# RWKV's triangular inverse by doubling: two chunks' products on four 64x64 tiles of TensorE, half of them written across the partition halves

## The reference, cut to what matters

```
def step(S, inp):
    r_t, w_t, k_t, v_t, kk_t, a_t = inp
    S = (S * w_t[:, :, None, :]
         - jnp.einsum('bhvk,bhk->bhv', S, kk_t)[..., None] * (kk_t * a_t)[:, :, None, :]
         + v_t[..., None] * k_t[:, :, None, :])
    return S, jnp.einsum('bhvk,bhk->bhv', S, r_t)
```

## Time and profile before

| | us |
|---|---|
| median of 3 runs | 1801.77 |
| lowest and highest | 1799.81, 1803.62 |
| profiled execution, device time | 1798.85 |
| its span, first to last instruction | 1797.2 |
| TensorE busy | 1711.3 (95%) |
| VectorE busy | 568.5 (32%) |
| ScalarE busy | 402.5 (22%) |
| mean granted clock of TensorE | 0.985 |

### The profile page before, as it was taken

The page is one execution under the profiler, slowest core; times in us unless marked ns, Lnnn a source line. Parts: engine busy times, 40 slices in busy tenths (PEclk is TensorE's granted clock), DMA queues, the critical chain, the costliest instruction groups (busy, mean ns, idle before and its releaser), DMA issues.

```text
span 1797.2 us, 27278 instructions
## 1 busy us (share of the span) xinstructions
PE 1711.3 (95%) x10992; PEld 1276.2 (71%) x10992; DVE 568.5 (32%) x1302; ACT 402.5 (22%) x899; POOL 125.5 (7%) x214
## 2 busy tenths in 40 slices
PE   7998899999999999999999989999999998999997
PEld 5675667677767777777766756676777676777775
DVE  1341464332024163330034314733220331533201
ACT  3221242131133231110132212412311332211101
POOL 1013000010010010000010130000000110000000
PEclk9999999999999999999999998999999999999999
DMA  9537222283447333333174272312734573343331
GB/s 350 172 116 253 112 96 72 71 319 118 149 148 307 126 123 141 134 132 126 68 254 162 84 255 106 119 49 83 298 126 144 194 274 119 118 141 131 131 117 50
DMA packets 64464, 273.54 MB, mean 152 GB/s; under 512 B 8529, under 2 KB 32530, under 8 KB 37074
## 3 DMA queue, kind: packets, MB, share of 16 engines
q1 hardware_dynamic: 51266, 208.57, 32.2%
q0 software_dynamic: 12512, 61.94, 9.2%
q10 hardware_dynamic: 560, 1.30, 0.2%
HBM read 262.58 MB, written 9.19 MB: 151 GB/s over the span
## 4 chain that ended last, share of the span: by engine, by line
PE 84%; DVE 6%; DMA 3%; issue 3%; ACT 3%; SPq 2%; POOL 0%; ACTq 0%; DVEq 0%; POOLq 0%
PE banks L815 42%; PE banks L844 15%; PE banks L766 5%; PE banks L822 5%; PE banks L799 4%; PE banks L873 3%; PE banks L763 3%; DVE work L1940 2%; PE banks L771 1%; DMA work<-in_ml_n 1%; PE banks L1072 1%; DVE o_branches L1940 1%; PE banks L1474 1%; PE banks L1493 1%; SPq L597 1%
## 5 line engine op out<-in xcount | busy, mean ns | idle before, releaser
L815 PE MATMUL banks<-h_normed,weight_ring 128*128 128x288 f32 x1888 | 459.4, 406 | 1.1 <-ACT h_normed L1558 1.1
L815 PEld LDWEIGHTS banks<-h_normed,weight_ring 128*128 128x128 f32 x1888 | 358.6, 190 | 100.5 <-ACT h_normed L1558 1.5
L844 PE MATMUL banks<-h_normed,weight_ring 128*128 128x288 f32 x1024 | 282.0, 419 | 4.6 <-ACT values_by_token L1723 4.6
L844 PEld LDWEIGHTS banks<-h_normed,weight_ring 128*128 128x128 f32 x1024 | 190.0, 192 | 61.1 <-ACT values_by_token L1723 7.0
L815 PE MATMUL banks<-work,weight_ring 128*128 128x288 f32 (+1 forms) x960 | 226.8, 399 | 1.8 <-issue 1.8
L815 PEld LDWEIGHTS banks<-work,weight_ring 128*128 128x128 f32 x960 | 182.2, 190 | 46.1 <-issue 2.6
L1940 DVE TENSOR_TENSOR squares<-squares 128x288 f32<-128x288 f32 (+2 forms) x40 | 20.3, 508 | 329.4 <-ACT squares L1596 329.3
L799 PE MATMUL banks<-h_normed,weight_ring 128*128 128x288 f32 x448 | 117.1, 411 | 2.3 <-ACT projected L1558 2.3
L1558 ACT ACTIVATE work<-banks 128x32 f32<-128x32 f32 (+8 forms) x142 | 55.9, 393 | 235.4 <-PE banks L766 62.0
L799 PEld LDWEIGHTS banks<-h_normed,weight_ring 128*128 128x128 f32 x448 | 82.2, 190 | 27.4 <-issue 4.3
L873 PE MATMUL banks<-h_normed,weight_ring 128*128 128x288 f32 x288 | 79.8, 434 | 20.9 <-DMA weight_ring<-in_w 13.8
(11 more groups left out here) (307 smaller groups left out, 1657.4 us busy)
## 6 DMA issues: line engine op xcount, KB each, us to landing
weight_ring<-in_w SPq DMA_DIRECT2D x171, 1024.0 KB, 4.8
work<-in_pool SPq DMA_DIRECT2D x112, 144.0 KB, 3.3
work<-in_mem_k POOLq DMA_DIRECT2D x12, 1024.0 KB, 11.6
work<-in_mem_v POOLq DMA_DIRECT2D x12, 1024.0 KB, 9.2
work<-in_pool POOLq DMA_DIRECT2D x64, 144.0 KB, 3.8
weight_ring<-in_pool SPq DMA_DIRECT2D x48, 144.0 KB, 3.0
projected<-in_mem_k POOLq DMA_DIRECT2D x4, 1024.0 KB, 25.6
projected<-in_mem_v POOLq DMA_DIRECT2D x4, 1024.0 KB, 5.8
```

Of the source, the lines that this page charges most:

```text
L815: last = mm(ps[:, bank, 0:width], block_of(first + k), rhs(k), start=k == 0, stop=k == n - 1)
L844: last = mm(ps[:, BANK[g], 0:N], block_of(t[2] + k), H[:, k, :] if t[0] == "gate" else O[:, 2 * n + k, :], start=k == 0, stop=k == t[3] - 1)
```

## The change

Both tiles' products of a level pair are issued together, and half of them go to the other half of the partitions, so that all four 64x64 tiles of the array are in use.

- `rw_x`: tile 0's products are written to their own half, tile 1's to the other half (`crossed`). ScalarE brings tile 1's X back with two copies of 64x256 instead of one of 128x256.
- `rw_y`: the products for T stay in their own half; those for the transpose are written to the other half, into bank 0 (tile 0) or 1 (tile 1). VectorE brings them back with two sums of 64x256 (`rw_turned_adds`), and T is summed by one of 128x256.
- the last level (`rw_y_last`): as `rw_x`, tile 1's products are written to the other half, and its sum onto T is made by two of 64x256.
- VectorE's order: the masks of the next two steps come first, then the transposes' four sums, then T's two, then `up_out`. `rw_x` waits for the transposes' sums (a new semaphore, `rw_tm`) and for both masks, `rw_y` for T's sums of the pair before.
- TensorE waits once, ahead of the loop, until banks 0 and 1 have been read (`rw_tokc`). The samples' step has functions of its own and does the same as before.

The number of products, their sizes and the mixing blocks between them stay.

```
                     def rw_x(level):
-                        j, i = RW_LEVELS[level]
-                        n, bank = min(TT[i][1], CH), RW_BANKS[i][0]
-                        pe.wait_ge(*at("rw_off", level + 1))
+                        for j, i in RW_LEVELS[level:level + 2]:
+                            pe.wait_ge(*at("rw_off", level + 1 + i))
+                        if level:
+                            pe.wait_ge(*at("rw_tm", level))
                         for h in range(4):
-                            for s in chunks_of(i):
-                                last = put(ps[s, bank, h * n:(h + 1) * n], r_off[i][s, h, 0:n], r_tm[i][s, h, 0:n])
-                        last.then_inc(S("rw_x"), 1)
+                            for s in chunks_of(0):
+                                for i, out in ((0, s), (1, crossed(s))):
+                                    last = put(ps[out, RW_BANKS[i][0], h * CH:(h + 1) * CH], r_off[i][s, h, :], r_tm[i][s, h, :])
+                                    if h == 3 and s.start:
+                                        last.then_inc(S("rw_x"), 1)
                     def rw_y(level):
...
+                        if level > 1:
+                            pe.wait_ge(*at("rw_t", level - 1))
                         for h in range(4):
+                            c = slice(h * CH, (h + 1) * CH)
                             for s in chunks_of(i):
...
+                                put(ps[s, RW_BANKS[i][1], c], r_x[i][s, h, :], r_tt[i][s, h, :])
+                                last = put(ps[crossed(s), i, c], r_tt[i][s, h, :], r_x[i][s, h, :])
+                        last.then_inc(S("rw_y"), 1)
+                    def rw_y_last(level):
+                        pe.wait_ge(*at("rw_xc", level + 2))
+                        pe.wait_ge(*at("rw_t", level))
+                        for h in range(4):
+                            for s in chunks_of(0):
+                                for i, out in ((0, s), (1, crossed(s))):
+                                    last = put(ps[out, RW_BANKS[i][1], h * CH:(h + 1) * CH], r_x[i][s, h, :], r_tt[i][s, h, :])
+                                    if h == 3 and s.start:
+                                        last.then_inc(S("rw_y"), 1)
...
                     for level in range(0, 10, 2):
                         rw_x(level)
-                        rw_x(level + 1)
                         mix(104 + 2 * level)
-                        rw_y(level)
-                        rw_y(level + 1)
+                        if level in RW_LAST:
+                            rw_y_last(level)
+                        else:
+                            rw_y(level)
+                            rw_y(level + 1)
                         mix(106 + 2 * level)
...  (ScalarE)
-                        copy(r_x[i][0:n, :, 0:m], ps[0:n, RW_BANKS[i][0], 0:4 * m].rearrange("p (h s) -> p h s", h=4), "rw_xc")
+                        src = ps[:, RW_BANKS[i][0], 0:4 * m].rearrange("p (h s) -> p h s", h=4)
+                        if i == 1:
+                            copy(r_x[1][0:CH, :, :], src[CH:P])
+                            copy(r_x[1][CH:P, :, :], src[0:CH], "rw_xc")
+                        else:
+                            copy(r_x[i][0:n, :, 0:m], src[0:n], "rw_xc")
...  (VectorE)
+                    def rw_turned_adds(level):
+                        j, i = RW_LEVELS[level]
+                        wait("rw_y", level + 1)
+                        for to, of in ((0, CH), (CH, 0)):
+                            half = r_tm[i][to:to + CH, :, :]
+                            tt(half, half, by_head(ps[of:of + CH, i, 0:4 * CH], CH), ADD, "rw_tm" if to else None)
...
-                    for level in range(10):
-                        rw_adds(level)
+                    for level in range(0, 10, 2):
                         if level < 8:
                             rw_offs(level + 2)
-                        if level in (1, 5):
+                            rw_offs(level + 3)
+                            rw_turned_adds(level)
+                            rw_turned_adds(level + 1)
+                        rw_adds(level)
+                        rw_adds(level + 1)
+                        if level in (0, 4):
                             up_out()
```

More of the change, by code:

```diff
@@ L248 @@
         (12, "rows_free"),
+        (8, "rw_tm"),
         (11, "rw_off rw_t rw_x rw_xc rw_y"),
@@ L1297, in chunks_of, with crossed @@
                         return [slice(0, NS)] if i == 2 else [slice(0, CH), slice(CH, P)]
+                    def crossed(s):
+                        return slice(CH - s.start, P - s.start)
                     def rw_x(level):
-                        j, i = RW_LEVELS[level]
-                        n, bank = min(TT[i][1], CH), RW_BANKS[i][0]
-                        pe.wait_ge(*at("rw_off", level + 1))
+                        for j, i in RW_LEVELS[level:level + 2]:
+                            pe.wait_ge(*at("rw_off", level + 1 + i))
+                        if level:
+                            pe.wait_ge(*at("rw_tm", level))
@@ L1308, in rw_y @@
                     def rw_y(level):
                         j, i = RW_LEVELS[level]
-                        n, bank = min(TT[i][1], CH), RW_BANKS[i][1]
                         pe.wait_ge(*at("rw_xc", level + 1))
+                        if level > 1:
+                            pe.wait_ge(*at("rw_t", level - 1))
                         for h in range(4):
+                            c = slice(h * CH, (h + 1) * CH)
                             for s in chunks_of(i):
-                                last = put(ps[s, bank, h * n:(h + 1) * n], r_x[i][s, h, 0:n], r_tt[i][s, h, 0:n])
-                            for s in () if level in RW_LAST else chunks_of(i):
-                                last = put(ps[s, bank, (4 + h) * n:(5 + h) * n], r_tt[i][s, h, 0:n], r_x[i][s, h, 0:n])
+                                put(ps[s, RW_BANKS[i][1], c], r_x[i][s, h, :], r_tt[i][s, h, :])
+                                last = put(ps[crossed(s), i, c], r_tt[i][s, h, :], r_x[i][s, h, :])
@@ new lines, in rw_x_samples, with rw_y_samples @@
+                    def rw_x_samples():
+                        pe.wait_ge(*at("rw_off", 11))
+                        for h in range(4):
+                            last = put(ps[0:NS, RW_BANKS[2][0], h * NS:(h + 1) * NS], r_off[2][0:NS, h, 0:NS], r_tm[2][0:NS, h, 0:NS])
+                        last.then_inc(S("rw_x"), 1)
+                    def rw_y_samples():
+                        pe.wait_ge(*at("rw_xc", 11))
+                        for h in range(4):
+                            last = put(ps[0:NS, RW_BANKS[2][1], h * NS:(h + 1) * NS], r_x[2][0:NS, h, 0:NS], r_tt[2][0:NS, h, 0:NS])
@@ L1338, in _ @@
                     mix(102)
+                    pe.wait_ge(*at("rw_tokc", 4))
                     for level in range(0, 10, 2):
                         rw_x(level)
-                        rw_x(level + 1)
                         mix(104 + 2 * level)
-                        rw_y(level)
-                        rw_y(level + 1)
+                        if level in RW_LAST:
[3 more added lines that the diff above has]
+                            rw_y(level + 1)
                         mix(106 + 2 * level)
@@ L1389, in _ @@
                     mix(148)
-                    rw_x(10)
+                    rw_x_samples()
                     mix(150)
-                    rw_y(10)
+                    rw_y_samples()
                     mix(152)
@@ L2316, in rw_offs, with by_head @@
                         j, i = RW_LEVELS[level]
+                        if 1 < level < 10:
+                            wait("rw_x", level - 1)
                         tt(tile_of(r_off, i), tile_of(r_at, i), mask(i, "level_c", 4, j), MUL, "rw_off")
+                    def by_head(ap, m):
+                        return ap.rearrange("p (h t) -> p h t", h=4)
+                    def rw_turned_adds(level):
[4 more added lines that the diff above has]
+                            tt(half, half, by_head(ps[of:of + CH, i, 0:4 * CH], CH), ADD, "rw_tm" if to else None)
                     def rw_adds(level):
@@ L2322, in rw_adds @@
                         wait("rw_y", level + 1)
-                        k = 4 if level in RW_LAST else 8
-                        tt(inverses(i, k), inverses(i, k), ps[0:n, RW_BANKS[i][1], 0:k * m].rearrange("p (k t) -> p k t", k=k), ADD, "rw_t")
+                        src = ps[:, RW_BANKS[i][1], 0:4 * m]
+                        if level == 9:
+                            for to, of in ((0, CH), (CH, 0)):
+                                half = r_tt[i][to:to + CH, :, :]
+                                tt(half, half, by_head(src[of:of + CH], m), ADD, "rw_t" if to else None)
+                        else:
+                            tt(tile_of(r_tt, i), tile_of(r_tt, i), by_head(src[0:n], m), ADD, "rw_t")
                     rw_masks(0)
```

## The result

The changed kernel takes 1793.14 us in the median of 9 runs (1790.95 to 1800.2), the kernel before 1801.77 us in 9 runs (1798.67 to 1807.03). The two medians lie 8.6 us apart. The ratio of the runs is 0.996 (95% interval 0.9946 to 0.9974): faster by 0.4%, which is 7.2 us, and between 4.7 and 9.7. The forecast was 1794.0 us, 7.8 us less than before; that the median lies only 0.9 us from it is finer than these runs can tell. The profiled execution after took 1792.38 us (span 1790.7), against 1798.85 (1797.2).

What follows compares the result with a forecast made beforehand. The doubling stage was taken as bounded by what TensorE issues: 6.44 us saved less 2.52 us of waits is 3.92 us per layer, 7.8 us over two layers, giving 1794.0 us; range 1789.5 to 1799.5.

Steps and rivals of the forecast that it cites:

- The products on four tiles: TensorE's X, Y and last Y groups shrink to 0.62, 1.09 and 0.62 us, saving 6.44 us per layer before waits.
- Rival 2: In X and Y, crossed products don't overlap with own-half ones, which keep 1.08 and 2.01 us; 1803.3 us, chance 0.07.
- The price of a half sum: A VectorE half sum of 64x256 before X costs as a whole one, 0.42 us, bounds 0.27 and 0.94.
- Rivals 3 and 4: VectorE's half sums cheaper, 0.27 us, giving 1789.9 (chance 0.05); or dearer, at 0.94 us giving 1812.5 (chance 0.05).
- The wait before X: TensorE, through Y and the mixing blocks, waits 0.39 us for VectorE's four half sums, four times per layer.
- The wait behind pair 4's `up_out`: Two `up_out` instructions at pair 4 delay VectorE's next masks and sums, 0.19 us more wait, once per layer.
- X to Y: ScalarE's three copies after X stay hidden with 0.27 us to spare; only the last Y waits, 0.35 us.
- `rw_bg`: After the last Y, TensorE waits 0.42 us for VectorE's one whole and two half sums.
- The sum: Gain of 3.92 us per layer, stage 22.28 us; 7.8 us over both layers, 1794.0 us against the median.
- Kept behind the stage: After the stage, TensorE's unchanged order and the transfers move along, so the whole gain is kept.
- Rival 5: Half or all of the gain is given back later by a transfer that doesn't move along; 1798 to 1802, chance 0.09.

Runs made afterwards that it cites:

- the uncrossed control: Changed kernel with every product written to its own partition half, same order, half copies and half sums; ratio 1.0004 to the kernel before, stage 27.24 us.
- Y alone: Kernel before with only Y crossed (half sums by VectorE), X as before; ratio 0.9963 to the kernel before, stage 23.19 and 22.70 us.
- X alone: Kernel before with only X crossed (half copies by ScalarE), Y as before; ratio 0.9974 to the kernel before, stage 24.69 and 24.43 us.
- the tile stored crossed: Changed kernel with tile 0's matrix and transposed inverse kept on the other half from `rw_pairs` on, X waiting on one semaphore; 1792.22 us, ratio 0.9939.
- the fastest kernel: As the tile stored crossed, with one mixing block behind X, three behind Y in full rounds, one moved ahead of `rw_bg`; 1787.81 us, ratio 0.9919.

## Why the prediction was right, step by step

- **The products on four tiles** (0.62, 1.09, 0.62 us; 6.44 per layer): 0.63, 1.09, 0.63. `rw_pairs` and the state products of the trace before were the right rows. Rival 2, the products of one row strip in turn, is refuted by the trace after and by the uncrossed control, which is 4.6 us slower in the stage. The prediction took 30 ns per record in the state products as a sign of two tiles side by side, and the row for one tile alone, which it lacked, is in the trace before: four products that all lie on one 64x64 tile, 8 records in 0.60 us (314.27 to 314.87), less the 0.15 are 56 ns per record.

```profile
314.27 0.67 PE L1362 MATMUL banks<-work 64*64 64x64 f32 x8
314.87 1.24 PE L844 MATMUL banks<-h_normed,weight_ring 128*128 128x288 f32 x4
```

  The Trainium skill's rule (TensorE: Matmul & The Clock Gate, "The mechanism"), of weight loads that overlap only for another row group, isn't what these traces show for 64x64 float32 tiles: the state products, of one row group and two column groups, went side by side, at 30 ns per record where one tile alone takes 56.
- **The price of a half sum** (0.42, bounds 0.27 and 0.94): 0.420 for 36 of them. Rivals 3 and 4 fall; reading one half and writing the other costs VectorE nothing here. ScalarE's half copy was put at 0.41 and is 0.379.
- **The wait before X** (0.39 each): 0.50. This is the term that I mis-sized. I took TensorE to start 0.05 us behind VectorE, from a place with one semaphore; before X, where three are waited for, it is 0.14. The run with a single wait shows it: the wait is 0.41 there. VectorE's later start, 0.83 instead of 0.81, is the other 0.02.
- **The wait behind pair 4's `up_out`** (0.39 + 0.19 = 0.58): 0.57 in the second layer. The total is right and its parts aren't: it is 0.50 + 0.07. From X(6) to X(8) VectorE's work sets the time (4.63 us, forecast and measured), and TensorE's longer lag stands at both ends and drops out.
- **X to Y** (hidden; 0.35 before the last Y): hidden, and 0.25. Three copies take 1.21 and not 1.29 us, because of the half copy's price.
- **`rw_bg`** (0.42): 0.40.
- **The sum:** stage 22.28 forecast, 22.63 and 22.53 measured, 22.28 with the single wait. Part of the closeness is luck: three waits before X were 0.33 us longer in all than forecast, and the last Y's was 0.10 shorter. The gain is 7.2 us for 7.8.
- **Kept behind the stage:** yes, to 0.2 us in 1446. Rival 5 falls.

What the prediction did not see is that X's crossing was worth almost nothing. It priced the steps in a row, X's saving first (2.30 us) and then the wait before X (1.75 us with the pair 4), and never asked what the wait would be without that saving. The total held, since both were counted, but X's crossing was credited with a gain of its own. The run with Y alone shows it: an X of 1.08 us in two groups covers the wait by itself.

Open: the gap in Y of pair 6, "issue" in the profile where it is named. It is in the first layer of the changed kernel (0.61 us), of X alone (0.26), of Y alone (0.61) and of the tile stored crossed (0.32), in no second layer, and not in the changed kernel's second profile. So the order of the program alone doesn't make it, and the profile shows no semaphore behind it. Its cause isn't known.

## What to carry to other kernels

A saving on one engine is worth the smaller of itself and the slack of what the next step waits for: before pricing an edit, ask what the wait behind it would be without the edit. Where work for TensorE can be cut by writing to other partitions, put the crossing in the storage (keep one operand on the other half from the start) rather than in copies and sums that bring results back; the first cost TensorE no time here and the second 0.42 us per half sum. And when independent blocks cover two waits, deal them out by the lengths of the waits, not evenly.

## What the runs showed beside this

**Four 64x64 tiles** take 32 float32 products in 1.09 us, two in 2.01; two products in a row on the same tile cost 0.05 us per group against alternating ones (X 1.13 for 1.08, Y 2.06 for 2.01, in two runs).

**The spread between executions is elsewhere.** But for the open gap the stages repeat to 0.1 us, while single runs of one kernel differ by up to 11 us (1798.29 to 1809.30 for the kernel before). The profiled execution of the fastest kernel is its slowest, 1792.21 us; windows of it, then of the changed kernel, from the same distance behind the first state product (592 us) to `rw_pairs(1)` of the second layer:

```profile
900.00:1168.33 268.33, 252.08 (x1977) 178.27 (x1975) 108.43 (x237) 66.63 (x143) 31.44 (x58) 0.92 0.44 151
```

```profile
903.00:1165.76 262.76, 242.75 (x1974) 172.12 (x1972) 108.50 (x238) 66.80 (x143) 31.94 (x58) 0.97 0.45 156
```

This stretch takes 5.6 us more at a granted clock of 0.92 against 0.97, though the change does not touch it. So a gain of 2 us is read from the stage of a profile, where it stands out, and not from the whole time.
